# Prompt attention of a decoder step: the turned weights one job further from their scores, small tiles' weights copied by ScalarE, one reciprocal for three jobs

## The chip, the cores and the metric

The kernel runs on one core of a Trainium2 chip. The metric is the device time of one execution in microseconds (us); lower is better. Engines are called by the profile's names: PE is TensorE, PEld its weight load, DVE VectorE, ACT ScalarE, POOL GpSimd, SP the engine that issues most DMAs.

## The reference, cut to what matters

One layer of a hybrid decoder over 1024 prompt tokens and 64 sampled tokens. After a large input projection the prompt goes through two attentions, and only those touch this change:

```python
# branch A: 12 query heads = 3 groups (window, dilation) x 4 slots, 4 K/V heads
for g, (win, dil) in enumerate(((128, 1), (512, 4), (2048, 16))):
    o, lse = dilated_band_group(qg[:, :, g], k_a, v_a, win, dil)   # softmax over strided keys
o_a = merge_groups(outs, lses)          # average, weights = softmax denominators
# branch B: 8 query heads, 2 K/V heads, softmax over the 256 best causal keys of an indexer
sc = where(kpos <= qpos, index_scores(q_i, k_i, w_i), -inf); idx = top_k(sc, 256)
o_b = sparse_attend(q_b, k_b[idx], v_b[idx])
```

The rest (input projection, indexer and its top-k, the sampled tokens' attention over caches, the gated output projections) is untouched.

## The kernel before, in words

The program is one hand-ordered stream per engine, with semaphores between them. The prompt attention runs in the profile from 2161 to 2541 us, after the input projection and the selection of keys and before the sampled tokens' attention.

Queries are taken in 8 blocks of 128 rows (i = 0 to 7). A block has 12 jobs in four triples: one job of branch A (one head slot, all three groups in one score tile) and two of branch B (one head each). So there are 96 jobs (`JOBS`), numbered n. A B job has i+1 key tiles of 128 columns; an A job has three strips together of 3 to 15 tiles, up to 1920 columns.

A job goes through these stages:

- `scores(n)` on PE (L670): query times keys into one of the score bank groups. Score banks are shared, so that `scores(n)` waits until the exponential of job n-2 is done (`exps_before`).
- On DVE the mask and the row maximum: one custom instruction in place for wide tiles (L605), or a TENSOR_REDUCE and a small TENSOR_SCALAR (L609, L611) where i is small; there the mask is added by PE (L675, L678).
- On ACT the exponential with its row sum, out of PSUM into one of three buffers `p_buf[n % 3]` (L531).
- For A jobs only, two or three additions on POOL that add the three groups' weights into one set by key (L559).
- `turn_weights(n, half)` on PE (L692): transposes of up to four key tiles into the one bank `T_BANK`. A block with more than four key tiles has a second half.
- A copy from `T_BANK` to `p_t`: the first half by DVE (L585), the second by ACT (L527).
- `values(n)` on PE (L703) into `O_BANK`.
- On DVE the reciprocal of the row sum (L617) and the scaling of the output into `o_tok` (L622).
- After each triple `turn_outputs(x)` on PE (L712) transposes the three outputs into the other part of `O_BANK`, and DVE copies them to `o_t` (L592, L593). SP stores `o_t` once a block.

Step n of PE's order is: first half of `turn_weights(n-2)`; `turn_outputs` if a triple is due (n = 3x+6, so ahead of an A job's scores); `scores(n)`; second half of `turn_weights(n-2)`; `values(n-3)`. DVE's step n is: the copy of job n-2's first half; the copies of a due triple; mask and maximum of n; reciprocal and scaling of n-3, which waits for `values(n-3)`. ACT's is: the copy of n-2's second half if there is one; the exponential of n. `values(n)` also waits for DVE to have scaled n-1 (`o_out`) and to have copied the last turned outputs (`ot_out`), since they share `O_BANK`. The exponential of n waits until job n-3 has been turned, since they share a `p_buf`.

Of the kernel before, what the change touches and what calls it, by code (L numbers as in the profile page):

```python
# [23 lines left out]
P = 128  # L24
# [95 lines left out]
def need(eng, sem, value):  # L120

    if not (isinstance(value, int) and value <= 0):
        eng.wait_ge(sem, value)


def decode_step(nc, ins, outs, scr):
    ctx = ExitStack()
    with ctx:
# [8 lines left out]
        banks = ctx.enter_context(nc.psum_tensor("banks", [P, 8, 512], F32))  # L137
# [232 lines left out]
        p_t = at("p_t", [P, 2, SEQ], F32, A0 + 89600)  # L370
# [7 lines left out]
        lsum = at("lsum", [P, 96], F32, A0 + 135168)  # L378
        rinv = at("rinv", [P, 96], F32, A0 + 135552)
# [49 lines left out]
        T_BANK, O_BANK = 6, 7  # L429

        USES = []
        for n in range(2, NJ + 2):
            USES.append(("w", n - 2, 0))
            if blocks_of(n - 2) > 4:
                USES.append(("w", n - 2, 1))
        use_no = {u: x for x, u in enumerate(USES)}
        triple_due = lambda n: (n - 4) // 3 if n >= 4 and (n - 4) % 3 == 2 else None

        def group_sums(n):

# [71 lines left out]
        def act_attention(act):  # L512

            columns_stored(act)
            for t in range(TT):
                rows = ROWS_OF(t)
                act.wait_ge(kv_turned, t + 1)
                b0 = 4 * (t % 2)
                nc.scalar.copy(k_tok[0:rows, t, 0:HA * HD], banks[0:rows, b0, :]).then_inc(kv_act, 1)
                nc.scalar.copy(v_tok[0:rows, t, 0:HA * HD], banks[0:rows, b0 + 1, :]).then_inc(kv_act, 1)  # L520
            act.wait_ge(small_in, 96)
            nc.scalar.copy(mask_b[:], mask_f[:]).then_inc(mask_cast, 1)  # L522
            for n in range(NJ + 2):
                m = n - 2
                if ("w", m, 1) in use_no:
                    act.wait_ge(t_done, use_no["w", m, 1] + 1)
                    nc.scalar.copy(p_t[:, m % 2, 512:blocks_of(m) * P], banks[:, T_BANK, 0:(blocks_of(m) - 4) * P]).then_inc(t_out, 1)  # L527
                if n < NJ:
                    act.wait_ge(nmx_set, n + 1)
                    need(act, t_done, 0 if n < 3 else last_use(n - 3) + 1)  # L530
                    nc.scalar.activation(p_buf[n % 3][:, 0:width_of(n)], flat(s_bank(n), P, width_of(n)), ACT.Exp,  # L531
                                         bias=nmx[:, n:n + 1], scale=-1.0 if in_place(n) else SCALE,
                                         accum_out=lsum[:, n:n + 1]).then_inc(exp_done, 1)
            act_sample(act)
# [34 lines left out]
        def dve_attention(dve):  # L569
            columns_stored(dve)  # L570
            for t in range(TT):
                rows = ROWS_OF(t)
                dve.wait_ge(kv_turned, t + 1)
                b0 = 4 * (t % 2) + 2
                nc.vector.tensor_copy(k_tok[0:rows, t, 512:768], banks[0:rows, b0, 0:256]).then_inc(kv_dve, 1)
                nc.vector.tensor_copy(v_tok[0:rows, t, 512:768], banks[0:rows, b0, 256:512]).then_inc(kv_dve, 1)
                nc.vector.tensor_copy(ki_tok[0:rows, t, :], banks[0:rows, b0 + 1, 0:ID]).then_inc(kv_dve, 1)
            dve.wait_ge(mask_cast, 1)
            for n in range(NJ + 4):
                m = n - 2  # L580
                if 0 <= m < NJ:
                    dve.wait_ge(t_done, use_no["w", m, 0] + 1)
                    need(dve, pv_done, m - 1)
                    w = min(4, blocks_of(m)) * P
                    nc.vector.tensor_copy(p_t[:, m % 2, 0:w], banks[:, T_BANK, 0:w]).then_inc(t_out, 1)  # L585
                if triple_due(n) is not None:
                    x = triple_due(n)
                    i, a = x // HA, x % HA
                    if a == 0:
                        need(dve, att_stored[i % 2], 16 * (i // 2))  # L590
                    dve.wait_ge(ot_done, x + 1)
                    nc.vector.tensor_copy(o_t[:, i % 2, a, :], banks[:, O_BANK, P:2 * P])  # L592
                    nc.vector.tensor_copy(o_t[:, i % 2, HA + 2 * a:HA + 2 * a + 2, :],  # L593
                                          banks[:, O_BANK, 2 * P:4 * P].rearrange("p (m n) -> p m n", m=2)).then_inc(ot_out, 1)
                if n < NJ:
                    kind, i, _ = JOBS[n]
                    dve.wait_ge(s_done, n + 1)
                    src = flat(s_bank(n), P, width_of(n))
                    if in_place(n):
                        if kind == "A":  # L600
                            mask = mask_b[:, (QT - 1 - i) * P:15 * P]
                        else:
                            dve.wait_ge(keep_cast, i - 1)
                            mask = keep_b[:, i % 2, 0:(i + 1) * P]
                        nc.vector.tensor_tensor_reduce(out=src, in0=src, in1=mask, scale=-SCALE, scalar=-TAKEN,  # L605
                                                       op0=ALU.add, op1=ALU.min, accum_out=nmx[:, n:n + 1])\
                            .then_inc(nmx_set, 1)
                    else:
                        nc.vector.tensor_reduce(mx[:, n:n + 1], src, AX, ALU.max).then_inc(mx_set, 1)  # L609
                        dve.wait_ge(mx_set, sum(not in_place(k) for k in range(n + 1)))  # L610
                        nc.vector.tensor_scalar(nmx[:, n:n + 1], mx[:, n:n + 1], -SCALE, None, ALU.mult)\  # L611
                            .then_inc(nmx_set, 1)
                m = n - 3
                if 0 <= m < NJ:
                    kind, i, h = JOBS[m]
                    dve.wait_ge(exp_done, m + 1)
                    nc.vector.reciprocal(rinv[:, m:m + 1], lsum[:, m:m + 1]).then_inc(rinv_set, 1)  # L617
                    dve.wait_ge(pv_done, m + 1)
                    dve.wait_ge(rinv_set, m + 1)
                    need(dve, ot_done, HA * (i - 1))  # L620
                    c0 = (h if kind == "A" else HA + h) * HD
                    nc.vector.tensor_scalar(o_tok[:, i % 2, c0:c0 + HD], banks[:, O_BANK, 0:HD], rinv[:, m:m + 1],  # L622
                                            None, ALU.mult).then_inc(o_out, 1)
            dve_sample(dve)

        def pe_attention(pe):
# [56 lines left out]
            def turn_weights(n, half):  # L683
                x = use_no["w", n, half]
                if JOBS[n][0] == "A":
                    early = half == 0 and JOBS[n][1] >= 5
                    pe.wait_ge(groups_added, sums_before(n) + (1 if early else len(group_sums(n))))
                else:
                    pe.wait_ge(exp_done, n + 1)
                need(pe, t_out, x)  # L690
                for b in range(4 * half, min(4 * half + 4, blocks_of(n))):
                    tr = nc.tensor.transpose(banks[:, T_BANK, b % 4 * P:(b % 4 + 1) * P],  # L692
                                             p_buf[n % 3][:, b * P:(b + 1) * P], ident[:])
                tr.then_inc(t_done, 1)

            def values(n):
                kind, i, h = JOBS[n]
                pe.wait_ge(t_out, last_use(n) + 1)
                need(pe, o_out, n)
                need(pe, ot_out, n // 3)  # L700
                c0 = h * HD if kind == "A" else (HA + h // (HB // KVB)) * HD
                for b in range(blocks_of(n)):
                    mm = nc.tensor.matmul(banks[:, O_BANK, 0:HD], p_t[:, n % 2, b * P:(b + 1) * P],  # L703
                                          v_tok[:, b, c0:c0 + HD], start=(b == 0), stop=(b == blocks_of(n) - 1))
                mm.then_inc(pv_done, 1)
# [7 lines left out]
                                             o_tok[:, i % 2, m * P:(m + 1) * P], ident[:])  # L713
                tr.then_inc(ot_done, 1)

            for n in range(NJ + 4):
                if 2 <= n < NJ + 2:
                    turn_weights(n - 2, 0)
                if triple_due(n) is not None:
                    turn_outputs(triple_due(n))  # L720
                if n < NJ:
                    scores(n)
                if ("w", n - 2, 1) in use_no:
                    turn_weights(n - 2, 1)
                if 3 <= n < NJ + 3:
                    values(n - 3)
            pe_sample(pe)


# [1343 lines left out]
```

## Time and profile before

| | us |
|---|---|
| median of 3 runs | 3461.18 (3458.52 to 3462.34) |
| the profiled execution | 3460.39 |
| its span, first to last instruction | 3458.8 |
| prompt attention in it, about 2161 to 2541 | 380 |
| PE busy in those 380 us | 331 |

The profile is of one execution. Part 2 of its page shows PE busy 97 % or more from slice 4 to 25 (the input projection) and from slice 33 on (the output projections). Between them lie the prompt attention (slices 25 to 29) and the sampled tokens (30, 31). A job's instructions can be found in the timeline by their tile sizes: 128x1920 is an A job of block 7, 128x1024 either a B job of block 7 or an A job of block 2.

### The profile page before, as it was taken

The numbers are of one execution on the slowest core, as the hardware profiler recorded it, in microseconds if no ns is written. First come the engines' busy times: TensorE is split into PE (matmuls) and PEld (weight loads), VectorE is DVE, ScalarE is ACT, GpSimd is POOL, SyncE is SP. The second block draws the span as 40 slices with busy tenths as digits, with TensorE's granted clock in tenths as the row PEclk, the third lists the DMA queues.
The fourth block names the chain that finished last, engine by engine and source line by source line (L and its number), as shares of the span: only waits on it lengthen the run. The fifth ranks groups of instructions, "written<-read, shape, count | busy, mean of one in ns | idle before, by whom it ended". The sixth has DMA issues, their size and how long they took to land. (4 is left out here: it accounts for less than half of the span.)

```text
span 3458.8 us, 52598 instructions
## 1 busy us (share of the span) xinstructions
PE 3242.1 (94%) x20665; PEld 3028.1 (88%) x20676; DVE 1738.8 (50%) x2537; ACT 743.1 (21%) x1166; POOL 251.7 (7%) x409
## 2 busy tenths in 40 slices
PE   5878999999999999999999997789988899999997
PEld 4656999999999999999999997557755699999997
DVE  4554778701333356455555543555533454554654
ACT  4221000011000111211111111223422233433432
POOL 3000000000000000000000000112113201000000
PEclk8999999999999999999999999899988899999998
DMA  9722222222212223232332324621247677494672
GB/s 322 247 87 88 64 79 74 62 70 72 74 56 74 84 59 112 74 105 87 91 104 75 111 80 153 179 60 41 61 139 222 208 224 203 148 276 129 201 206 79
DMA packets 522864, 422.03 MB, mean 122 GB/s; under 512 B 19835, under 2 KB 491131, under 8 KB 519491
## 3 DMA queue, kind: packets, MB, share of 16 engines
q1 hardware_dynamic: 500044, 338.53, 34.3%
q0 software_dynamic: 22720, 82.20, 6.3%
q8 instruction: 59, 0.97, 0.1%
q14 instruction: 41, 0.34, 0.0%
HBM read 346.96 MB, written 75.81 MB: 122 GB/s over the span
## 5 line engine op out<-in xcount | busy, mean ns | idle before, releaser
L278 PE MATMUL banks<-h_hi,w_hi 128*128 128x352 f32 (+2 forms) x3744 | 1226.7, 328 | 12.2 <-DVE w_lo L269 10.2
L280 PE MATMUL banks<-h_hi,w_lo 128*128 128x352 f32 (+2 forms) x3744 | 1222.0, 326 | 0.0
L279 PE MATMUL banks<-h_lo,w_hi 128*128 128x352 f32 (+2 forms) x3744 | 1221.1, 326 | 0.0
L278 PEld LDWEIGHTS banks<-h_hi,w_hi 128*128 128x128 f32 (+1 forms) x3744 | 701.5, 187 | 17.1 <-issue 15.8
L279 PEld LDWEIGHTS banks<-h_lo,w_hi 128*128 128x128 f32 (+1 forms) x3744 | 703.8, 188 | 1.3
L280 PEld LDWEIGHTS banks<-h_hi,w_lo 128*128 128x128 f32 (+1 forms) x3744 | 700.7, 187 | 1.3
L269 DVE TENSOR_TENSOR w_lo<-w_raw,w_hi 128x2048 fp32r<-128x2048 f32 (+1 forms) x79 | 180.0, 2279 | 640.7 <-ACT w_hi L265 532.2
L1527 DVE MAX8 best<-work 128x8 f32<-128x1088 f32 x224 | 289.3, 1292 | 10.8 <-issue 1.0
L304 ACT ACTIVATE col<-banks 128x384 f32<-128x384 f32 x150 | 71.2, 475 | 1027.6 <-PE banks L280 1027.6
L1529 DVE MATCH_REPLACE8 work<-best,work 128x1088 f32<-128x1088 f32 x224 | 285.9, 1276 | 0.0
L265 ACT CAST w_hi<-w_raw 128x2048 fp32r<-128x2048 f32 (+1 forms) x79 | 149.9, 1897 | 582.9 <-PE banks L280 538.5
L1477 PE MATMUL banks<-m_hi,u_hi 128*128 128x384 f32 (+1 forms) x768 | 254.0, 331 | 1.6 <-DVE u_lo L1358 1.5
L1479 PE MATMUL banks<-m_hi,u_lo 128*128 128x384 f32 (+1 forms) x768 | 250.5, 326 | 0.0
L1478 PE MATMUL banks<-m_lo,u_hi 128*128 128x384 f32 (+1 forms) x768 | 250.2, 326 | 0.0
L1358 DVE TENSOR_TENSOR u_lo<-u_raw,u_hi 128x1536 fp32r<-128x1536 f32 (+1 forms) x96 | 196.5, 2047 | 62.5 <-ACT u_hi L1305 62.3
L1305 ACT CAST u_hi<-u_raw 128x1536 fp32r<-128x1536 f32 (+1 forms) x96 | 162.7, 1696 | 287.8 <-PE banks L1479 275.1
L319 DVE TENSOR_TENSOR rot_b<-banks,rot_sin 64x384 f32<-64x384 f32 (+3 forms) x186 | 99.1, 533 | 212.6 <-PE banks L280 208.5
L1477 PE MATMUL banks<-o_hi,u_hi 128*128 128x384 f32 (+1 forms) x576 | 188.7, 328 | 1.2 <-DVE u_lo L1358 1.2
L1478 PE MATMUL banks<-o_lo,u_hi 128*128 128x384 f32 (+1 forms) x576 | 188.3, 327 | 0.0
L1479 PE MATMUL banks<-o_hi,u_lo 128*128 128x384 f32 (+1 forms) x576 | 188.3, 327 | 0.0
L1697 POOL DMA_DIRECT2D scratch_proj<-col x76 | 40.4, 532 | 1752.0 <-ACT col L304 1126.5
L670 PE MATMUL banks<-k_t,q_tile 128*128 128x512 f32 (+3 forms) x464 | 163.1, 475 | 3.2 <-ACT mask_b L522 3.0
(239 smaller groups left out, 3355.4 us busy)
## 6 DMA issues: line engine op xcount, KB each, us to landing
w_raw<-in_w_in SPq DMA_DIRECT2D x78, 1024.0 KB, 5.7
u_raw<-in_w_out SPq DMA_DIRECT2D x96, 512.0 KB, 5.3
scratch_proj<-col POOLq DMA_DIRECT2D x78, 544.0 KB, 3.0
ada_w<-in_w_ada SPq DMA_DIRECT2D x16, 2048.0 KB, 14.5
u_raw<-in_w_pb SPq DMA_DIRECT2D x48, 512.0 KB, 4.7
gate_w<-in_w_ada SPq DMA_DIRECT2D x16, 1024.0 KB, 7.7
u_raw<-in_w_pa SPq DMA_DIRECT2D x48, 256.0 KB, 3.2
gates<-scratch_proj SPq DMA_DIRECT2D x64, 192.0 KB, 2.4
```

Source lines behind the costliest of these rows:

```text
L269: nc.vector.tensor_tensor(w_lo[:, par, :, 0:width], w_raw[:, :, 0:width], w_hi[:, par, :, 0:width], ALU.subtract).then_inc(w_lo_set, 1)
L278: nc.tensor.matmul(dst, w_hi[:, par, k, 0:width], h_hi[:, k, a:b], start=(k == 0), stop=False)
L279: nc.tensor.matmul(dst, w_hi[:, par, k, 0:width], h_lo[:, k, a:b], start=False, stop=False)
L280: mm = nc.tensor.matmul(dst, w_lo[:, par, k, 0:width], h_hi[:, k, a:b], start=False, stop=(k == KT - 1))
L670: mm = nc.tensor.matmul(dst, lhs, k_t[:, kh, key0 + a - at_col:key0 + b - at_col], start=True, stop=in_place(n))
L1305: nc.scalar.copy(u_hi[u % 2][:, 0:ks, :], u_raw[:, u, 0:ks, :]).then_inc(u_hi_set, 1)
L1358: nc.vector.tensor_tensor(u_lo[u % 2][:, 0:ks, :], u_raw[:, u, 0:ks, :], u_hi[u % 2][:, 0:ks, :], ALU.subtract).then_inc(u_lo_set, 1)
L1477: nc.tensor.matmul(dst, u_hi[par][:, k, :], hi[:, k, 0:n], start=(k == ks[0]), stop=False)
L1478: nc.tensor.matmul(dst, u_hi[par][:, k, :], lo[:, k, 0:n], start=False, stop=False)
L1479: mm = nc.tensor.matmul(dst, u_lo[par][:, k, :], hi[:, k, 0:n], start=False, stop=(k == ks[-1]))
L1527: nc.vector.max(best8[:], work[:])
L1529: nc.vector.match_replace(work[:], best8[:], work[:], TAKEN)
```

## The change

The job whose weights are turned at step n becomes n-3 (LAG = 3), the values n-4, and a triple's outputs are turned at step 3x+7, so ahead of the scores of the first B job. Where a block has at most four key tiles (i = 0 to 3) the copy to `p_t` goes from DVE to ACT, ahead of the exponential in ACT's step. DVE takes the reciprocals of a triple in one instruction, before the scaling of its first job.

```diff
+        LAG = 3
+        triple_due = lambda n: (n - LAG - 2) // 3 if n >= LAG + 2 and (n - LAG - 2) % 3 == 2 else None
+        last_step = NJ + LAG + 2
@@ act_attention
-            for n in range(NJ + 2):
-                m = n - 2
+            for n in range(NJ + LAG):
+                m = n - LAG
+                if 0 <= m < NJ and blocks_of(m) <= 4:
+                    act.wait_ge(t_done, use_no["w", m, 0] + 1)
+                    need(act, pv_done, m - 1)
+                    w = blocks_of(m) * P
+                    nc.scalar.copy(p_t[:, m % 2, 0:w], banks[:, T_BANK, 0:w]).then_inc(t_out, 1)
@@ dve_attention
-            for n in range(NJ + 4):
-                m = n - 2
-                if 0 <= m < NJ:
+            for n in range(last_step):
+                m = n - LAG
+                if 0 <= m < NJ and blocks_of(m) > 4:
...
-                m = n - 3
+                m = n - LAG - 1
                 if 0 <= m < NJ:
                     kind, i, h = JOBS[m]
-                    dve.wait_ge(exp_done, m + 1)
-                    nc.vector.reciprocal(rinv[:, m:m + 1], lsum[:, m:m + 1]).then_inc(rinv_set, 1)
+                    if m % 3 == 0:
+                        dve.wait_ge(exp_done, m + 3)
+                        nc.vector.reciprocal(rinv[:, m:m + 3], lsum[:, m:m + 3]).then_inc(rinv_set, 1)
+                        dve.wait_ge(rinv_set, m // 3 + 1)
                     dve.wait_ge(pv_done, m + 1)
-                    dve.wait_ge(rinv_set, m + 1)
@@ pe_attention
-            for n in range(NJ + 4):
-                if 2 <= n < NJ + 2:
-                    turn_weights(n - 2, 0)
+            for n in range(last_step):
+                m = n - LAG
+                if 0 <= m < NJ:
+                    turn_weights(m, 0)
                 if triple_due(n) is not None:
                     turn_outputs(triple_due(n))
                 if n < NJ:
                     scores(n)
-                if ("w", n - 2, 1) in use_no:
-                    turn_weights(n - 2, 1)
-                if 3 <= n < NJ + 3:
-                    values(n - 3)
+                if ("w", m, 1) in use_no:
+                    turn_weights(m, 1)
+                if 0 <= m - 1 < NJ:
+                    values(m - 1)
```

## Rows read from the trace of the kernel before

**Rows 1.** The page, part 1: busy us (share of the span) and instructions.

```profile
PE 3242.1 (94%) x20665; PEld 3028.1 (88%) x20676; DVE 1738.8 (50%) x2537; ACT 743.1 (21%) x1166; POOL 251.7 (7%) x409
```

**Rows 2.** Windows: length; busy PE, PEld, DVE, ACT, POOL; granted clock; DMA; GB/s.

```profile
2161.00:2222.00 61.00, 43.78 (x232) 33.75 (x232) 33.75 (x125) 16.14 (x50) 9.90 (x17) 0.80 0.48 150
2222.00:2263.00 41.00, 31.76 (x174) 23.61 (x175) 22.61 (x66) 9.67 (x24) 7.41 (x9) 0.92 0.63 166
2263.00:2313.00 50.00, 40.67 (x206) 27.59 (x209) 27.52 (x73) 12.57 (x26) 8.60 (x9) 0.93 0.19 52
2313.00:2367.00 54.00, 45.20 (x255) 34.40 (x253) 28.14 (x68) 15.75 (x34) 10.53 (x13) 0.94 0.16 45
2367.00:2541.00 174.00, 169.63 (x1056) 130.30 (x1055) 99.71 (x215) 65.94 (x112) 33.94 (x42) 1.00 0.17 50
```

**Rows 3.** Waits in 2161:2541, PE's: us in total, times, longest.

```profile
PE banks L692 <- POOL p_buf L559: 33.8, 22, 2.7
PE banks L703 <- issue: 6.7, 11, 1.0
PE banks L712 <- DVE o_tok L622: 4.0, 10, 0.6
...
PE banks L692 <- DVE p_t L585: 2.4, 6, 0.9
```

**Rows 4.** Timeline, PE, block 2: outputs turned; start, us.

```profile
2232.70 0.81 PE L712 MATMUL banks<-ident,o_tok 128*128 128x128 f32 x3
...
2244.18 0.55 PE L712 MATMUL banks<-ident,o_tok 128*128 128x128 f32 x3
...
2253.94 0.55 PE L712 MATMUL banks<-ident,o_tok 128*128 128x128 f32 x3 [0.19 <-DVE o_tok L622]
```

**Rows 5.** Timeline, block 2, around one A job's scores; brackets: idle before.

```profile
2251.56 0.55 PE L692 MATMUL banks<-ident,p_buf 128*128 128x128 f32 x3 [1.64 <-POOL p_buf L559]
...
2256.55 0.83 PE L703 MATMUL banks<-v_tok,p_t 128*128 128x128 f32 x6
2256.76 1.22 DVE L609 TENSOR_REDUCE mx<-banks 128x1 f32<-128x1024 f32 x1 [1.60 <-PE banks L675]
2257.22 0.49 PE L692 MATMUL banks<-ident,p_buf 128*128 128x128 f32 x3
2257.55 0.81 PE L670 MATMUL banks<-k_t,q_tile 128*128 128x384 f32 x2
...
2258.33 0.35 DVE L622 TENSOR_SCALAR o_tok<-banks,rinv 128x128 f32<-128x128 f32 x1
```

**Rows 6.** Timeline, blocks 4 (2322, 2336) and 5 (2396).

```profile
2322.06 1.12 PE L692 MATMUL banks<-ident,p_buf 128*128 128x128 f32 x4 [2.69 <-POOL p_buf L559]
...
2336.28 0.66 PE L692 MATMUL banks<-ident,p_buf 128*128 128x128 f32 x4 [1.68 <-POOL p_buf L559]
...
2396.52 1.46 PE L670 MATMUL banks<-k_t,q_tile 128*128 128x512 f32 x4
...
2396.80 0.35 DVE L622 TENSOR_SCALAR o_tok<-banks,rinv 128x128 f32<-128x128 f32 x1
```

**Rows 7.** Lines by form, 2161:2541: busy us, mean ns; idle before.

```profile
L617 DVE RECIPROCAL rinv<-lsum 128x1 f32<-128x1 f32 x96 | 15.0, 156 | 0.0
L593 DVE COPY o_t<-banks 128x256 f32<-128x256 f32 x31 | 12.9, 415 | 0.0
L592 DVE COPY o_t<-banks 128x128 f32<-128x128 f32 x31 | 8.9, 287 | 4.2 <-PE banks L712 3.8 <-issue 0.3
...
L585 DVE COPY p_t<-banks 128x256 f32<-128x256 f32 x12 | 5.0, 418 | 5.2 <-PE banks L692 5.2
L527 ACT COPY p_t<-banks 128x256 f32<-128x256 f32 x12 | 4.4, 369 | 21.3 <-PE banks L692 21.3
```

**Rows 8.** Timeline, PE, after the stage: sampled tokens' keys.

```profile
2560.58 1.75 PE L1030 MATMUL banks<-ident,win_k 128*128 128x128 f32 x7 [7.50 <-DMA pool_k<-in_cache_k]
```

More of the change, by code:

```diff
@@ L431, in decode_step @@
         USES = []
[L432 to L435, printed above, removed]
+        for m in range(NJ):
+            USES.append(("w", m, 0))
+            if blocks_of(m) > 4:
+                USES.append(("w", m, 1))
         use_no = {u: x for x, u in enumerate(USES)}
-        triple_due = lambda n: (n - 4) // 3 if n >= 4 and (n - 4) % 3 == 2 else None
+        LAG = 3
+        triple_due = lambda n: (n - LAG - 2) // 3 if n >= LAG + 2 and (n - LAG - 2) % 3 == 2 else None
+        last_step = NJ + LAG + 2
         def group_sums(n):
@@ L578, in dve_attention @@
             dve.wait_ge(mask_cast, 1)
-            for n in range(NJ + 4):
-                m = n - 2
-                if 0 <= m < NJ:
+            for n in range(last_step):
+                m = n - LAG
+                if 0 <= m < NJ and blocks_of(m) > 4:
                     dve.wait_ge(t_done, use_no["w", m, 0] + 1)
                     need(dve, pv_done, m - 1)
-                    w = min(4, blocks_of(m)) * P
+                    w = 4 * P
                     nc.vector.tensor_copy(p_t[:, m % 2, 0:w], banks[:, T_BANK, 0:w]).then_inc(t_out, 1)
```

## The prediction

> **What bounds the kernel now.** I read in this order: the page's busy shares, the busy times by stretch, PE's waits in the attention stage, then the timeline of single triples. PE is busy for 94% of the span [rows 1], but the change touches only the 380 us from 2161 to 2541. There the reader is to see two halves. In blocks 5 to 7 PE is busy 169.6 of 174 us and the clock is granted in full. In blocks 0 to 4 it is busy 161.4 of 206 us, and the granted clock is 0.80, then 0.92 to 0.94 [rows 2]. DVE is busy at about half there, ACT at a quarter, POOL less: nobody is full, the stage waits on a chain. Its link is named by the waits: of 46.9 us in which PE's attention instructions wait, 33.8 are `turn_weights` waiting for POOL's sum of an A job's three groups, 22 times; 6.7 are values behind DVE, 4.0 turned outputs waiting for the scaled output, 2.4 second halves waiting for DVE's copy [rows 3]. The 22 are nearly all in blocks 0 to 4, one per triple: with small tiles PE has too little other work in the two steps between an A job's scores and its turning.
>
> Outside 2161 to 2541 nothing is edited. What follows hangs on the stage's end: SP starts the next loads once the last outputs are stored, and PE then waits 7.50 us for pool_k [rows 8]. That wait stays, and slides along with the stage. SP's own order of loads and POOL's of casts are not moved past anything. So what the stage gains, the kernel gains, up to what the clock does later.
>
> **The change part by part.**
>
> *Three jobs of distance.* PE does the same instructions in another order. At the step where it now waits for POOL it turns a B job whose exponential has long ended; the A job follows one step later, after another 0.8 us of scores and 0.7 of values in block 2 and more in later blocks. The wait in block 2 is 1.64 [rows 5], in block 4 it is 1.68 and once 2.69 [rows 6]; a step of PE's (turn, scores, values: 0.33 + 0.65 + 0.67, by the distances of starts in rows 5, the scores taken like the ones before 2252.59) covers the first, and in block 4 a step is over 3 us. So the 33.8 us of POOL waits go to about nothing. No new wait for the exponential arises from the step order: `scores(n)` still needs exp(n-2), and PE now has the turning of n-3 ahead of it and not that of n-2.
>
> *What is late next.* The turned outputs of a triple now fall at the step after an A job's scores. DVE's order in the A step is mask and maximum of n, and only then the scaling of n-4, the last output of the triple. `turn_outputs` therefore waits behind the longest reduction of the triple, where it stood behind that of a B job. Block 2, counting from PE's start of the values (2256.55) in rows 5: values to 2257.22, turning to 2257.55, and there `turn_outputs` would start; the scaling starts at 2258.33 now, 0.13 earlier without the reciprocal before it, and lasts 0.35: 2258.55, plus 0.05 to be seen, 2258.6. PE waits 1.05. Then come the turned outputs (0.39, from 2253.94 to the scores in that triple, an estimate), B scores of 0.65, and values that share the bank with the turned outputs: DVE's copies begin 0.2 after the transposes, take 0.29 + 0.42 [rows 7], and end some 0.3 after the scores. In all 1.35 per triple, and of the present waits in such a triple (1.64, the 0.19 of rows 4, and the values behind DVE, of which rows 3 have 11 with 6.7 us) nothing stays. In block 5 the same reading is: turning over at 2396.52, scaling over at 2396.80 + 0.35 = 2397.15, less 0.1 for the reciprocal, plus 0.05: a wait of 0.6 where there is none now [rows 6]; B scores of over 1.1 us hide the copies.
>
> The other blocks I set between these. Block 1: 1.6 (its reduction is shorter, but so is PE's cover, and the copies show longer). Block 3: 1.1. Block 4: 0.8. Blocks 6 and 7, where the values are longer: 0.4 and 0.2. With four triples each that is 6.4 + 5.4 + 4.4 + 3.2 + 2.4 + 1.6 + 0.8 = 24.2 us of new waits. Bounds of this term: 0, if DVE scales in time everywhere, and 32 triples at 1.35, 43 us.
>
> *The rest of the idle time.* Block 0 has about 5 of the 46.9 us; there everything is short and I leave it as it is. At the end the pipeline drains one step longer: a turn's second half waits for DVE's copy with no scores between, some 0.9 more beside the 1.6 there now. So after: 24.2 + 5 + 2.5 = 31.7 against 46.9, a gain of 15.2 us.
>
> *The copies.* 48 jobs lose a DVE copy (128x256: 418 ns) and get an ACT copy (369 ns) [rows 7]. ACT has room [rows 2], but the copy stands behind exp(n-1) in its queue, and what is queued behind it is exp(n). PE's next turning waits for it (one bank). In block 2 the chain of a B job, scores 0.8, seen 0.2, mask 0.7, exponential 0.8, copy 0.5, turning 0.35, with gaps 3.6 us, and of an A job some 6.3, is a ring over two steps: 6.3 + 2 x 3.6 = 13.5 us for two triples, while PE needs about 2 x 8.4. It is hidden, at zero; without that cover it would cost the copy, 0.5 us for each of 48 jobs, 24 us at most. The gain that DVE has from losing the copy, an earlier mask, is under 0.1 a step, since DVE now waits for PE before the mask [rows 5]; I take zero, and at most 48 x 0.1.
>
> *One reciprocal.* 64 instructions of 156 ns less [rows 7]. It is read in the step after the A job's, so the scaling that matters above loses the reciprocal ahead of it; that is in the sum. The wait for exp(n-2) at that place is already passed when DVE has reduced n. Elsewhere zero, at most 64 x 0.1 = 6 us.
>
> *The clock.* The granted clock in 2222 to 2367 means 2 x (0.08 x 41 + 0.07 x 50 + 0.06 x 54) = 20 us at 1.2 GHz, the rest at 2.4 GHz. The matmuls show where: four transposes take 1.12 us after the wait of 2.69 and 0.66 after one of 1.68 [rows 6]. A triple of block 2 takes 11.48 us with a slow stretch and 9.76 without [rows 4]: 1.7 for 3.4 us slow, so those 20 us cost 10. Another 24 us lie in blocks 0 and 1, mostly at the stage's start, where nothing much changes; I count 7 of them, worth 3. Of these 13 the change can give back all or nothing, or take more. PE's idle share in blocks 2 to 4 falls from 27 in 145 us to about 13; I take 8 back.
>
> The Trainium skill (TensorE: Matmul & The Clock Gate, "A second HAM failure mode: psum-queue depth-cycling") says that small idle spells between groups of matmuls are enough to make the clock swing. The trace agrees: no wait here reaches 3 us, and the clock falls in blocks 1 to 4. By that rule shorter but still regular waits need not restore it; that is the second rival, and pushed further the third.
>
> Sum: 15.2 + 8 = 23 us. On the profiled execution's own 3460.39 that is 3437.4; it stands 0.8 under the median of the runs, so I say 3438.
>
> **The rivals.**
>
> *The outputs aren't late.* If DVE's order hurts less than I read (half of the 24.2 gone) and the clock is full in blocks 1 to 4, 15 + 12 + 13 = 40: 3421. For it: the POOL waits precede the slow stretches that I can see. Against: rows 5 and 6 place the scaling after the turning with little doubt.
>
> *Waits change, the clock doesn't.* The 20 us stay slow, as the new waits keep PE idle for a tenth of its time: gain 15 or a little less, 3446. For it: a clock that drops in some triples and not in others with the same wait. Against: the 0.2 to 0.6 us waits of blocks 1 and 2 alone show no drop of their own.
>
> *Slower: the late outputs bring the clock down.* The place is `turn_outputs` behind the A job's reduction, now in all 32 triples, also in blocks 5 to 7, which run at 2.4 GHz with hardly a gap. If each of the 28 triples after block 0 gets a slow stretch at 1.7, that is 48 against the 13 of now: 35 lost, 15 gained, 3481. It is slower from (15 + 13) / 1.7 = 17 slow stretches on. Against: the new waits there are 0.2 to 0.6 where drops followed waits of 1.6 and more.
>
> *It does little.* The ring through ACT's copy is tighter than I drew it in blocks 0 to 3 (exponential, copy, turning, scores one behind the other), and each of 48 jobs gives back 0.3 to 0.5: 15 to 24 of the 23, 3453 to 3462. Against: PE's step is longer than the ring by a fifth.
>
> **How the numbers follow.** Chances: forecast 0.50 (3430 to 3444 by itself), outputs not late 0.13, clock stays 0.20, does little 0.10, slower 0.07. The range reaches from 3422 to 3453, which leaves out the slower case, most of the one that does little, and half of the fastest. A measurement of this kernel can tell 0.2%, 7 us. Faster than 3454: the first three and a little of the fourth, 0.85; within: 0.08; slower: 0.07.
>
> **What would show it.** Right: PE's wait for POOL under 4 us in the stage; a wait of `turn_outputs` for the scaling of about 1 us once a triple in blocks 1 to 3, and 0.2 to 0.8 in 4 to 7, in sum 20 to 30 us; granted clock 0.96 or more in blocks 2 to 4; copies to `p_t` 96 on ACT and 48 on DVE; the stage 357 us long and the sampled tokens' stage unchanged. Wrong: PE waiting for exponentials before scores, or for ACT's copies before turning; granted clock under 0.95 in blocks 5 to 7; a stage that shrinks without the total following.

## The result, and the profile after

The changed kernel takes 3414.03 us (median of 4 runs, 3409.52 to 3416.94) against 3461.76 for the one before (4 runs too), a ratio of 0.9861 with a 95% interval of 0.9844 to 0.9878: 47.7 us less. I had forecast 3438, so 23 less, with 3422 as the fast end of the range. The direction was right, the size half of what came.

The first view of after is the same table of stretches as [rows 2]. It is cut at block ends that come earlier now: blocks 0, 1, 2, 3, 4, and 5 to 7 (columns: length, busy time of PE, PEld, DVE, ACT, POOL, granted clock, DMA share, GB/s).

```profile
2163.00:2195.00 32.00, 24.05 (x135) 19.12 (x136) 15.29 (x54) 13.03 (x46) 5.59 (x11) 0.79 0.83 265
2195.00:2223.00 28.00, 23.34 (x150) 17.81 (x148) 15.51 (x48) 11.99 (x37) 6.65 (x9) 1.00 0.54 139
2223.00:2258.00 35.00, 30.65 (x179) 21.98 (x180) 17.87 (x49) 15.70 (x37) 7.83 (x9) 1.00 0.54 153
2258.00:2298.00 40.00, 36.93 (x216) 27.00 (x219) 20.71 (x50) 18.30 (x37) 9.22 (x10) 1.00 0.23 63
2298.00:2342.00 44.00, 42.00 (x270) 33.55 (x268) 28.87 (x61) 16.97 (x37) 10.69 (x13) 1.00 0.21 59
2342.00:2501.00 159.00, 154.37 (x974) 119.69 (x974) 89.43 (x171) 61.44 (x101) 30.79 (x39) 1.00 0.15 44
```

The reader is to see the column of the granted clock: 1.00 from block 1 on, where it was 0.92 to 0.94, so the 2.4 GHz level throughout. The stage, 380 us long before, is 338 now.

The second view is what PE waits for in the stage, the answer to [rows 3]:

```profile
PE banks L720 <- DVE o_tok L630: 17.7, 26, 1.2
PE banks L711 <- DVE o_t L600: 2.7, 8, 0.5
PE banks L700 <- DVE p_t L592: 2.1, 3, 0.9
PE banks L678 <- ACT p_buf L538: 1.0, 1, 1.0
...
PE banks L700 <- POOL p_buf L566: 0.2, 1, 0.2
```

POOL is gone from the list, 33.8 to 0.2 us. In its place stands what the prediction named: `turn_outputs` behind the scaling, 17.7 us, and the values behind the copies of the turned outputs, 2.7.

The third view is the timeline of a triple of block 2, the answer to [rows 5]:

```profile
2229.50 0.83 PE L711 MATMUL banks<-v_tok,p_t 128*128 128x128 f32 x6
2229.70 1.23 DVE L616 TENSOR_REDUCE mx<-banks 128x1 f32<-128x1024 f32 x1 [2.20 <-PE banks L683]
2230.17 0.49 PE L700 MATMUL banks<-ident,p_buf 128*128 128x128 f32 x3
...
2231.04 0.35 DVE L630 TENSOR_SCALAR o_tok<-banks,rinv 128x128 f32<-128x128 f32 x1
...
2231.45 0.55 PE L720 MATMUL banks<-ident,o_tok 128*128 128x128 f32 x3 [0.79 <-DVE o_tok L630]
...
2232.87 0.91 PE L711 MATMUL banks<-v_tok,p_t 128*128 128x128 f32 x6 [0.23 <-DVE o_t L600]
...
2239.76 0.44 PE L720 MATMUL banks<-ident,o_tok 128*128 128x128 f32 x2 [0.79 <-DVE o_tok L630]
```

The idle columns have 0.79 + 0.23 = 1.02 where I had worked out 1.05 + 0.3; why the two can't be set side by side stands below. The triple takes 2239.76 - 2231.45 = 8.31 us. In [rows 4] it took 9.76 at full clock and 11.48 with a slow stretch (a stretch at the lower of the clock's two levels, 1.2 GHz and not 2.4).

For the comparisons below I measure the stage from the first exponential of the prompt attention to the start of the last transpose of outputs, and the blocks between the exponentials of their first jobs, both read from the timeline:

| us | block 0 | 1 | 2 | 3 | 4 | 5 | 6 | 7 and end | stage |
|---|---|---|---|---|---|---|---|---|---|
| before | 26.0 | 35.9 | 42.3 | 49.0 | 54.8 | 49.0 | 55.7 | 64.2 | 376.9 |
| after | 21.3 | 26.9 | 33.2 | 39.0 | 42.8 | 48.4 | 54.2 | 68.5 | 334.3 |

40.2 of the 42.6 us are gained in blocks 1 to 4. Block 0 is 4.7 us shorter and the end 4.3 longer, which is in part one thing: with a distance of three, the turning and the values of one job more come behind the last exponential, and those of one job fewer fall into block 0.

The other 5 of the 47.7 us lie outside the stage. What comes behind it is not edited, yet it took 912 to 922 us in the profiles of this study; of the same changed kernel 914, 913 and 916. By the clock records of these traces 75 to 92 us of it ran at the lower level, mostly more where it was longer. Medians a few us apart therefore say less than the stage does.

### The profile page after: what moved, and what is told of

It is laid out like the page before. It is cut to its first block, busy times and chain, and to the rows that moved or that the text cites. A ratio compares the mean times of both kernels' runs of the same rounds, so it can differ in the third digit from the quotient of the medians.

```text
span 3415.4 us, 52518 instructions
## 1 busy us (share of the span) xinstructions
PE 3218.2 (94%) x20665; PEld 3015.6 (88%) x20676; DVE 1714.6 (50%) x2425; ACT 760.4 (22%) x1214; POOL 251.7 (7%) x409
## 4 chain that ended last, share of the span: by engine, by line
PE 89%; DMA 4%; DVE 3%; ACT 1%; issue 1%; SPq 1%; DVEq 0%; POOL 0%; ACTq 0%; POOLq 0%
PE banks L278 18%; PE banks L280 18%; PE banks L279 18%; PE banks L1486 6%; PE banks L1488 6%; PE banks L1487 6%; PE banks L678 4%; PE banks L711 3%; PE banks L700 1%; DMA ada_w<-in_w_ada 1%; PE banks L333 1%; DMA u_raw<-in_w_out 1%; PE banks L1039 1%; PE banks L2026 1%; PE banks L2022 1%
```

## The experiments

*Which part of the change did it.* Four kernels take the three edits apart.

e1 is the kernel before with the distance alone (cut to its one constant; the loops follow from it as in the change):

```diff
+        LAG = 3          # copies all on DVE, one reciprocal per job
```

> The kernel before with the distance of three jobs alone: DVE still copies small tiles, one reciprocal per job. Theory A (distance removes the POOL waits, and with them the stretches at 1.2 GHz in blocks 1 to 4): PE's wait for POOL under 1 us, granted clock 1.00 from block 1 on, 3418 to 3426 us, since turn_outputs waits some 0.1 to 0.25 us longer behind each reciprocal. Theory B (the copies on ACT and the joint reciprocal bring a third or more of the 47 us): 3430 or more.

3426.85 us (ratio 0.9890, 0.9867 to 0.9913), just above the range of theory A. The stage is 340.8 us, so 36 of the 42.6 us are gained, the granted clock is 1.00 from block 1 on, and POOL's wait is gone:

```profile
PE banks L714 <- DVE o_tok L624: 25.6, 29, 1.4
...
PE banks L694 <- POOL p_buf L561: 0.2, 1, 0.2
```

e4 is the opposite, the copies and the joint reciprocal without the distance:

```diff
-        LAG = 3
+        LAG = 2
```

> The changed kernel with the distance of two jobs: copies on ACT and joint reciprocals alone. Theory A: the POOL waits stay, 25 us or more in the stage, slow stretches in blocks 1 to 4 stay: 3450 to 3462 us. Theory B: 3430 to 3445.

3458.04 us (ratio 0.9987, 0.9977 to 0.9997), as theory A has it, stage 377.5 us. POOL's wait is all there:

```profile
PE banks L700 <- POOL p_buf L566: 35.0, 22, 2.7
PE banks L711 <- issue: 6.8, 12, 0.9
```

So the distance makes the gain; the other two edits without it leave the stage where it was (377.5 for 376.9).

e2 gives the changed kernel its single reciprocals back (cut):

```diff
-                    if m % 3 == 0:
-                        dve.wait_ge(exp_done, m + 3)
-                        nc.vector.reciprocal(rinv[:, m:m + 3], ...)
+                    dve.wait_ge(exp_done, m + 1)
+                    nc.vector.reciprocal(rinv[:, m:m + 1], ...)
...
```

> The changed kernel with one reciprocal per job again. Theory A: only the wait of turn_outputs behind the scaling grows, from 17.7 us by 26 to 31 times 0.1 to 0.25, so 3417 to 3422 us. If the reciprocal is hidden: 3412 to 3416. If it mattered in every step: over 3425.

3421.31 us (ratio 0.9880, 0.9856 to 0.9905), in the range of theory A. By the ratios alone it isn't apart from the changed kernel (0.9861, 0.9844 to 0.9878); the stage decides, 341.4 against 334.3: 7.1 us, and the output wait grows by as much, 17.7 to 24.9:

```profile
PE banks L719 <- DVE o_tok L629: 24.9, 29, 1.4
```

e3 gives the small tiles' copies back to DVE (cut):

```diff
-                if 0 <= m < NJ and blocks_of(m) <= 4:     # act_attention
-                    nc.scalar.copy(p_t[...], banks[:, T_BANK, 0:w])
-                if 0 <= m < NJ and blocks_of(m) > 4:      # dve_attention
+                if 0 <= m < NJ:
...
```

> The changed kernel with the small tiles' copy on DVE again. Theory A: 3413 to 3418 us, the copy lies beside the transposed outputs that DVE waits for anyway. Theory B: DVE's queue was what held blocks 0 to 3, 3422 or more, and PE waits longer for the scaled output there.

3415.99 us (ratio 0.9872, 0.9848 to 0.9895), as theory A has it. The stage is 332.8 us, blocks 1 to 4 equal to after's within 0.1 us each. The 1.5 us lie in block 0, where the granted clock is 0.87 here and 0.78 in after's profile. The copy's engine makes no difference in blocks 1 to 4.

*Whether the clock was the waits' doing.* e8 leaves the time until POOL's sum as it is, and lets PE work in it:

```diff
+                if JOBS[n][0] == "A" and half == 0 and 1 <= JOBS[n][1] <= 4:
+                    need(pe, t_out, x)
+                    for _ in range(10):
+                        nc.tensor.transpose(banks[:, T_BANK, 0:P], ident[:], ident[:])
                 if JOBS[n][0] == "A":
```

> The kernel before, distance two, with ten transposes of the identity into the free turning bank before PE waits for POOL's sum, for A jobs of blocks 1 to 4: the wait is as long as before, but PE works through 1.1 us of it. They compute nothing that is used. Theory C (the idle waits behind POOL are what lowered the clock, and the slow stretches of blocks 1 to 4 cost 13 us): at most two slow stretches in blocks 1 to 4, stage 10 to 14 us shorter, 3447 to 3453 us. Theory D (the clock there does not hang on these waits): slow stretches stay, 3459 to 3466 us.

3451.0 us (ratio 0.9966, 0.9952 to 0.9980), as theory C has it. PE's shown wait for POOL is halved, from 33.8 us:

```profile
PE banks L696 <- POOL p_buf L559: 17.5, 22, 2.4
```

Four stretches, blocks 1 to 4, granted clock third from the end:

```profile
2192.00:2232.00 40.00, 32.48 (x209) 25.07 (x208) 23.57 (x77) 10.35 (x28) 7.67 (x11) 0.97 0.38 108
2232.00:2272.00 40.00, 34.87 (x219) 26.07 (x219) 23.59 (x68) 10.51 (x24) 7.38 (x10) 1.00 0.60 155
2272.00:2318.00 46.00, 41.88 (x249) 30.18 (x249) 27.20 (x68) 12.22 (x24) 8.56 (x9) 1.00 0.20 55
2318.00:2370.00 52.00, 47.21 (x299) 37.15 (x300) 28.85 (x68) 16.56 (x36) 10.77 (x14) 1.00 0.18 50
```

The 0.97 comes from the end of block 0: block 1 begins at 2195.5, and from there on the clock is granted in full. Blocks 1 to 4 take 171.1 us instead of 182.1, though nothing was taken off the chain and 160 useless transposes came in. That nothing else changed is seen in the triples that had the full clock before: 8.20, 9.76, 11.45 and 12.85 us in blocks 1 to 4, and 8.21, 9.78, 11.47 and 12.86 here. So 10.9 us there were the price of the clock alone.

e5 goes the other way and makes the output wait of the changed kernel about as long as POOL's had been:

```diff
+                    if m % 3 == 2 and 2 <= i + 1 <= 4:
+                        nc.vector.tensor_reduce(mx[:, m:m + 1], mask_b[:, 0:1024], AX, ALU.max)
                     dve.wait_ge(pv_done, m + 1)
```

> The changed kernel with one more DVE instruction of about 1.1 us (a maximum over 1024 mask columns, unused) before a triple's last output is scaled, for jobs ahead of blocks 1 to 3 (12 times), so that turn_outputs waits 1.8 to 2.2 us. Theory C (one wait of that length brings a slow stretch now and then): 12 x 1.1 = 13 us of waits and 2 to 5 slow stretches of 1.7: 3430 to 3436 us. If the clock holds: 3426 to 3429. If the late outputs cost nothing: 3414.

3438.73 us (ratio 0.9931, 0.9915 to 0.9948). The added instruction takes 1.21 us, 12 times, 14.5 us. The waits, of 1.8 to 2.2 us, and the turned outputs after them in block 2 show both clock levels (0.55 and 0.87 for the same three transposes):

```profile
2251.38 0.55 PE L722 MATMUL banks<-ident,o_tok 128*128 128x128 f32 x3 [1.90 <-DVE o_tok L632]
2261.45 0.87 PE L722 MATMUL banks<-ident,o_tok 128*128 128x128 f32 x3 [2.16 <-DVE o_tok L632]
```

```profile
2190.00:2220.00 30.00, 21.86 (x133) 16.95 (x131) 17.57 (x46) 11.90 (x36) 5.38 (x9) 0.94 0.28 77
2220.00:2262.00 42.00, 33.78 (x177) 25.20 (x178) 21.59 (x52) 15.20 (x37) 7.82 (x10) 0.87 0.64 170
2262.00:2307.00 45.00, 37.37 (x205) 26.11 (x204) 23.80 (x53) 17.96 (x36) 8.55 (x10) 0.97 0.20 56
```

The stage is 20.2 us longer, 5.7 more than the added instructions: theory C again, with its time missed by 3 us. What about the waits decides, the length of one or how much idle time there is in all, these runs don't tell apart; both rose together. Waits of one length stand before both levels, here and in the kernel before, where those of 1.91 us in blocks 2 and 3 lie in triples of 11.45 us with a granted clock of 1.00 and in triples of 12.95 and 13.12 with 0.87.

*What the output wait is worth.* e6 lets DVE scale the triple's last output first, then reduce the A job (cut):

```diff
+                first = (n - LAG - 1) % 3 == 2 and n < NJ and JOBS[n][1] <= 3
+                if first:
+                    scale(n - LAG - 1)
...
```

> The changed kernel, in blocks 0 to 3, with the scaling of a triple's last output ahead of the A job's mask and maximum. Theory A (the wait of turn_outputs is DVE's order): the wait in blocks 1 to 3 falls from 0.7 to 1.1 to about 0.3, and 12 x 0.5 = 6 us go, 3407 to 3410 us. Rival: the A job's exponential is later by the values, 0.5 to 0.9 us, and PE waits for it before scores instead: 3413 to 3420.

3418.04 us (ratio 0.9874, 0.9858 to 0.9891), stage 336.7: a miss. The output wait falls to 7.2 us, but the values behind the turned outputs' copies take its place:

```profile
PE banks L717 <- DVE o_t L600: 9.8, 14, 0.8
PE banks L726 <- DVE o_tok L612: 7.2, 19, 0.8
PE banks L706 <- ACT p_t L531: 2.7, 10, 0.5
```

I read that as DVE's whole queue being what PE meets, not the place of one instruction in it; no run tests it by itself. The rival had the direction, but named the wrong wait: the one for exponentials before scores is 1.0 us, as it was.

e7 turns the outputs two steps later, before the next A job's scores (cut):

```diff
-        triple_due = lambda n: (n - LAG - 2) // 3 if ... (n - LAG - 2) % 3 == 2 else None
+        triple_due = lambda n: (n - LAG - 6) // 3 if ... (n - LAG - 6) % 3 == 0 else None
-                need(pe, ot_out, n // 3)                    # values
+                need(pe, ot_out, (n - 2) // 3)
-                pe.wait_ge(o_out, 3 * x + 3)                # turn_outputs
+                pe.wait_ge(o_out, min(3 * x + 5, NJ))
```

> The changed kernel with a triple's outputs turned two steps later (at step 3x+9, ahead of the next A job's scores, after the scaling of job 3x+4, with the values of job 3x+5 the first that wait for the copies). Theory A: of the 17.7 + 2.7 us that turn_outputs and the values behind it wait, all but 3 go: 3395 to 3400 us. Rival: PE's idle time only moves to the exponential or to POOL: 3408 or more.

3413.98 us (ratio 0.9866, 0.9849 to 0.9882), stage 332.6: another miss, nearest to the rival, though the wait moved to neither of the places it named.

```profile
PE banks L700 <- ACT p_t L531: 7.8, 15, 0.8
PE banks L711 <- issue: 4.0, 10, 0.7
...
PE banks L720 <- DVE o_tok L630: 1.9, 7, 0.4
```

The output wait is gone (1.9), and PE waits before turning for ACT's copy, which stands behind the A job's exponential. That is the ring of exponential, copy and turning that I had priced at zero, now the last to arrive. One slow stretch lies in block 1 as well (one triple of 8.05 us with a granted clock of 0.82, the next 6.65 with 1.00), 1.4 us of its stage. e9 takes the wait for ACT away by giving the copies back to DVE, on top of e7:

> The changed kernel with the outputs turned two steps later, as in the run before, and the small tiles' copy on DVE again. Theory A (there, with the output wait gone, PE's next wait is for ACT's copy behind the A job's exponential, 7.8 us in the stage, 0.56 once a triple in block 3): that wait goes, stage 325 to 330 us, 3401 to 3408 us. Rival: DVE's queue becomes the bound in its place, 3411 or more.

Its stage is 325.0 us, 9.2 under the changed kernel's, in the range of theory A, and the wait for ACT's copy is gone; what remains is small everywhere:

```profile
PE banks L706 <- issue: 4.2, 11, 0.7
PE banks L695 <- POOL p_buf L561: 3.8, 12, 0.6
...
PE banks L715 <- DVE o_tok L625: 1.3, 4, 0.4
```

Its time misses theory A's range and lies in the rival's, 3412.6 us (ratio 0.9854, 0.9837 to 0.9870), beside 3414.95 (0.9860, 0.9843 to 0.9876) of the changed kernel on the same chip:

> The changed kernel itself, on the same chip as the one beside it: 3411 to 3418 us.

Both ran once more together:

> The version with later outputs and DVE copies once more, on the same chip as the changed kernel. Its attention stage was 9 us shorter than the changed kernel's, its time only 2. If the rest of the kernel took the difference by chance: 3403 to 3409 us. If the part behind the stage is longer in each of its executions: 3410 to 3415.

> The changed kernel once more, beside the version with later outputs: 3411 to 3418 us, its stage 334 us from the first exponential as twice before.

3411.35 (0.9849, 0.9832 to 0.9866), the second of the two cases, against 3417.82 (0.9868, 0.9851 to 0.9885), stages 325.0 and 334.2. The version is ahead both times, by 2 and 6 us, with intervals that overlap, so that a gain over the changed kernel is shown for the stage alone; the 9 us are in part given back. Past the stage, the output projections (from the first split of their weights to the end) take 714 and 715 us in its two profiles, 708 to 710 in the changed kernel's three. Most of the difference is the clock: for the same 4178 matmuls PE is busy 685.4 and 685.5 us in the version and 681.1 in each of the three, and by the traces' clock records the lower level was granted for 30 us in the version and for 20 to 22 in the others. What lowers it there, no run shows.

## Why the prediction was wrong

*What bounded the kernel* was read rightly: PE's wait for POOL's sum, removed by the distance alone (e1), untouched by the rest (e4). The stage's gain did pass on to the end.

*"So the 33.8 us of POOL waits go to about nothing"*: right, 0.2.

*"In all 1.35 per triple ... 24.2 us of new waits"*: place and size were right, though the idle columns have less, 17.7 + 2.7 = 20.4, and 1.02 per triple in block 2, 0.46 in block 4, 0.26 in block 5. I had counted from where PE's next instruction would start; the columns count from where the last matmul is shown to end. In [rows 5] three transposes are shown from 2257.22 for 0.49 us, and the next instruction starts after 0.33: 0.16 less. Counted my way, the triple of block 2 above waits 2231.45 - (2230.17 + 0.33) = 0.95 for my 1.05 and 0.23 + 0.16 = 0.39 for my 0.3, in all 1.34. With 0.16 for each of the 34 waits, 20.4 becomes about 26 (an estimate). Block 4 has 0.62 for my 0.8 and block 5 0.42 for my 0.6. In block 2 my 1.05 was 0.1 too long, by the reciprocal: I took 0.13 off for it, and without it the scaling starts 2231.04 - 2229.70 = 1.34 us after the reduction, where that was 1.57 in [rows 5], so 0.23 less. e2 measures the same, 7.1 us over 31 triples.

*"So after: 24.2 + 5 + 2.5 = 31.7 against 46.9, a gain of 15.2 us"*: this is the step that failed. It takes waits counted from starts away from waits of the idle columns, which are 0.16 us short each, in some 50 waits [rows 3]. The triples show what really went. Here are one per block, 1 to 4, at full clock, before and then after (length, then PE's busy time):

```profile
2205.72:2213.92 8.20, 5.66 (x36) 4.32 (x36) 5.15 (x18) 2.12 (x7) 1.45 (x2) 1.00 0.00 0
2244.18:2253.94 9.76, 7.51 (x46) 5.58 (x46) 5.86 (x18) 2.36 (x6) 1.71 (x2) 1.00 0.37 110
2288.10:2299.55 11.45, 9.34 (x54) 6.35 (x53) 6.73 (x17) 2.71 (x5) 1.99 (x2) 1.00 0.00 1
2326.88:2339.73 12.85, 10.84 (x66) 8.38 (x66) 7.13 (x17) 4.24 (x11) 2.44 (x3) 1.00 0.22 62
2194.80:2201.43 6.63, 5.48 (x37) 4.30 (x37) 3.77 (x12) 2.98 (x10) 1.45 (x2) 1.00 0.41 121
2231.45:2239.76 8.31, 7.29 (x46) 5.55 (x47) 4.22 (x12) 3.76 (x10) 1.72 (x2) 1.00 0.58 175
2267.88:2277.80 9.92, 9.13 (x52) 6.33 (x53) 4.80 (x12) 4.51 (x10) 2.00 (x2) 1.00 0.00 1
2297.71:2308.50 10.79, 10.33 (x66) 8.24 (x66) 7.14 (x16) 4.20 (x10) 2.46 (x3) 1.00 0.25 74
```

They are 6.6 us shorter together, times four 26.4 us without any help of the clock. The idle columns account for 5.4 of the 6.6; the rest is PE shown as busy for longer with the same matmuls (10.84 against 10.33 in block 4). My sum had in effect taken, as the idle columns of these four before less my new waits, 2.54 - 1.6, 2.25 - 1.35, 1.91 - 1.1 and 2.01 - 0.8, together 3.9, times four 15.4. Of the 11 us between, by my estimate some 6 are the 0.16 of the waits before (three in a triple of blocks 1 and 2, two in one of 3 and 4), about 1.5 the new waits that came out shorter than forecast, and the rest delays too short for a row.

*"I take 8 back"* for the clock: this is the other mis-sized term. In blocks 1 to 4 11 us came back: e8 measures 10.9. The other way of counting agrees roughly: 40.2 us, less 26.4, is 13.8, of which 1 is the longer wait of [rows 6], and some of the rest comes with the edges of the blocks, which lie one job earlier in PE's order now. I discounted because shorter, regular waits remained. The runs show no slow stretch in blocks 1 to 7 in any of the three profiles of the changed kernel, with output waits of up to 1.2 us, and slow ones again with waits of 1.8 to 2.2 (e5). The rule of the Trainium skill that I cited (TensorE: Matmul & The Clock Gate, "A second HAM failure mode: psum-queue depth-cycling") agrees with the kernel before, whose waits for POOL in blocks 1 to 4 are 1.4 to 2.7 us; to the shorter waits left over I had stretched it, and there it was borne out only once, by the one slow stretch of e7. The slower rival, which lived on it, was never near.

*The copies* at zero: right for this change in blocks 1 to 4 (e3). The ring was real, and decided as soon as the output wait was gone (e7, e9). Its estimated size was off: I had it a fifth shorter than PE's step.

*The losses in blocks 5 to 7* (2.4 + 1.6 + 0.8 us) did not show: the triples there take 12.2, 13.6 and 15.2 us before and after, though those of block 5 have a wait of 0.26 now and no row of idle time before. With single reciprocals, block 5 takes 49.5 us instead of 48.4 (e2), so that the joint reciprocal paid for the later outputs there.

In sum the mechanism was right and two terms were too small: the idle time by 11 us and the clock by 3 in blocks 1 to 4, and both errors pointed one way. Of the other 10 us of the miss, 5 lie outside the stage and the rest in its ends and the edges of its blocks, not taken apart by any run. The rival nearest to the result was "the outputs aren't late" at 3421, in part by luck: it rightly took the full clock, but the outputs were as late as forecast, and the 12 us that it took off for them stood in for idle time that the sum had missed. Of my signs POOL's wait, the clock and the waits of `turn_outputs` in blocks 1 to 3 came as said; the sum of the latter was 17.7 us for my 20 to 30, by the idle columns, and the stage 338 us for my 357.

## What to carry to other kernels

- Where a wait recurs every few microseconds and the granted clock is under 1, price the slow stretches as part of that wait. Here nearly all of them were gained when waits of 1.4 to 2.7 us gave way to some of 1.2 and less; to check, fill the wait with useless work and see what returns (e8).
- A small instruction between a long one and the one that another engine waits for can be on the path each time, with its hand-over: a 156 ns reciprocal cost 0.23 us per triple (e2).
- Count waits before and after in one measure. PE's idle column begins where the last matmul is modelled to end, 0.16 us after the next could have started here; the distance of starts from triple to triple, at one clock, has all of it.
- When a wait is removed, the next one lies close by. Here it moved from POOL to the scaled output, and from there a few tenths at a time to the turned outputs' copies (e6) or to ACT's copy (e7); only two edits together (e9) shortened the stage by more than 2 us.

## What the runs showed of the hardware that was not expected

PE doing useless transposes in the wait was worth 11 us, 0.34% of the kernel, by the clock alone (e8). With waits of up to 1.2 us, 26 in the stage, the granted clock stayed at 1.00 from block 1 on in all three profiles of the changed kernel; with twelve waits of 1.8 to 2.2 us it fell to 0.87 to 0.97 in blocks 1 to 3 (e5). Short waits were no guarantee: in e7 a triple had 0.82 after one with waits of 0.72, 0.51 and 0.29 us. And a removed stall is worth more than its idle time in the rows: a triple of block 4 went from 12.85 to 10.79 us, 2.06 less, while its idle time went from 2.01 to 0.46, 1.55 less.
